# Two plain chunks instead of three in the FFN behind attention, and its root mean square taken two tiles earlier

## The reference, cut to what matters

```python
def rms_norm_2(x, g):
    y = x * lax.rsqrt(jnp.mean(x * x, axis=-1, keepdims=True) + 1e-6)
    return y * g

def swiglu(x, w_gate, w_up, w_down):
    return (jax.nn.silu(x @ w_gate) * (x @ w_up)) @ w_down

for l in range(2):                      # x is 512 tokens x 1024
    x = x + 0.5 * swiglu(rms_norm_2(x, ffn1_norm[l]), ...)      # FFN 1, hidden width 2816
    ...                                 # projections, forgetting attention, recurrence
    x = x + merged @ w_out[l]
    x = x + 0.5 * swiglu(rms_norm_2(x, ffn2_norm[l]), ffn2_w_gate[l], ffn2_w_up[l], ffn2_w_down[l])
```

## Time and profile before

| | |
|---|---|
| median of 3 runs | 3305.78 us (3305.65 to 3306.15) |
| profiled execution | 3305.81 us, of which the trace spans 3304.1 us |
| PE busy | 3288.7 us |
| DVE / ACT / POOL busy | 2273.0 / 1532.7 / 2197.9 us |
| FFN 2 of layer 0, its plain part | from 1763.79 us to the first fast matmul at 1851.32 us |
| one plain chunk of it | 1807.80 to 1840.44 us |
| one fast chunk of it | 1882.67 to 1913.28 us |

### The profile page before, as it was taken

The page is one execution under the profiler, slowest core; times in us unless marked ns, Lnnn a source line. Parts: engine busy times, 40 slices in busy tenths (PEclk is TensorE's granted clock), DMA queues, the critical chain, the costliest instruction groups (busy, mean ns, idle before and its releaser), DMA issues.

```text
span 3304.1 us, 54409 instructions
## 1 busy us (share of the span) xinstructions
PE 3288.7 (100%) x18310; PEld 2811.7 (85%) x18310; DVE 2273.0 (69%) x3503; ACT 1532.7 (46%) x2141; POOL 2197.9 (67%) x2139
## 2 busy tenths in 40 slices
PE   9999999999999999999999999999999999999999
PEld 5888778899889997788888899889987888888998
DVE  8887685988877878714435888778878334247887
ACT  4365664443443336735544333533347445534333
POOL 6443445877769886553356888689875544468896
PEclk9999999999999999999999999999999999999999
DMA  6221453322232223332223322233223222223232
GB/s 225 89 71 65 166 179 115 119 97 99 89 115 96 102 89 102 102 122 65 75 89 108 115 101 103 77 115 114 93 86 115 90 102 71 83 95 109 102 109 101
DMA packets 94488, 343.40 MB, mean 104 GB/s; under 512 B 10609, under 2 KB 11249, under 8 KB 93954
## 3 DMA queue, kind: packets, MB, share of 16 engines
q1 hardware_dynamic: 86978, 312.11, 27.5%
q10 hardware_dynamic: 7360, 29.29, 2.8%
HBM read 335.03 MB, written 2.13 MB: 102 GB/s over the span
## 4 chain that ended last, share of the span: by engine, by line
PE 85%; DVE 5%; POOL 4%; DVEq 2%; issue 2%; ACT 1%; DMA 0%; ACTq 0%; SPq 0%; POOLq 0%
PE ps L689 25%; PE ps L691 25%; PE ps L690 25%; POOL w_lo L635 3%; POOL t_lo L635 1%; PE ps L856 1%; PE ps L857 1%; PE ps L858 1%; PE ps L1391 1%; PE ps L1373 1%; PE ps L938 1%; PE ps L884 1%; DVE arena L2765 1%; PE ps L1382 1%; DVEq L2787 0%
## 5 line engine op out<-in xcount | busy, mean ns | idle before, releaser
L635 POOL TENSOR_TENSOR w_lo<-raw,w_hi 128x256 fp32r<-128x256 f32 (+1 forms) x1468 | 1306.3, 920 | 906.8 <-ACT w_hi L1479 905.1
L689 PE MATMUL ps<-a_hi,w_lo 128*128 128x512 f32 (+1 forms) x2728 | 1020.6, 374 | 1.1 <-POOL w_lo L635 0.7
L691 PE MATMUL ps<-a_hi,w_hi 128*128 128x512 f32 (+1 forms) x2728 | 1006.1, 369 | 0.0
L690 PE MATMUL ps<-a_lo,w_hi 128*128 128x512 f32 (+1 forms) x2728 | 1005.4, 369 | 0.0
L635 POOL TENSOR_TENSOR w_lo<-arena,w_hi 128x512 fp32r<-128x512 f32 x514 | 780.4, 1544 | 170.9 <-ACT w_hi L2078 114.6
L689 PEld LDWEIGHTS ps<-a_hi,w_lo 128*128 128x128 f32 x2728 | 513.4, 188 | 100.4 <-issue 18.0
L691 PEld LDWEIGHTS ps<-a_hi,w_hi 128*128 128x128 f32 x2728 | 512.4, 188 | 87.8
L690 PEld LDWEIGHTS ps<-a_lo,w_hi 128*128 128x128 f32 x2728 | 512.8, 188 | 80.8 <-issue 0.5
L1479 ACT ACTIVATE w_hi<-raw 128x1024 fp32r<-128x1024 f32 x321 | 336.6, 1053 | 324.5 <-PE ps L691 305.2
L689 PE MATMUL ps<-b_hi,w_lo 128*128 128x512 f32 (+1 forms) x1052 | 390.1, 371 | 0.6 <-POOL w_lo L635 0.2
L2078 ACT ACTIVATE w_hi<-arena 128x1024 fp32r<-128x1024 f32 x192 | 203.7, 1061 | 398.0 <-PE ps L691 398.0
(11 more groups left out here) (365 smaller groups left out, 4982.1 us busy)
## 6 DMA issues: line engine op xcount, KB each, us to landing
raw<-in_stream SPq DMA_DIRECT2D x419, 512.0 KB, 3.3
arena<-in_stream SPq DMA_DIRECT2D x148, 512.0 KB, 3.3
arena<-in_mod_w ACTq DMA_DIRECT2D x32, 512.0 KB, 4.2
arena<-in_mod_w SPq DMA_DIRECT2D x16, 512.0 KB, 11.6
arena<-arena ACTq DMA_DIRECT2D x16, 256.0 KB, 3.7
arena<-cum_rows ACTq DMA_DIRECT2D x2, 2048.0 KB, 9.6
xres<-in_x_t SPq DMA_DIRECT2D x4, 512.0 KB, 5.3
arena<-in_first SPq DMA_DIRECT2D x8, 256.0 KB, 11.8
```

The costliest lines, as they stand in the source:

```text
L635: last = pool.tensor_tensor(to[:, at], of[:, at], hi[:, at].bitcast(F32), ALU.subtract)
L689: pe.matmul(out, lo, x_hi, start=start, stop=False)
L690: pe.matmul(out, hi, x_lo, start=False, stop=False)
L691: return pe.matmul(out, hi, x_hi, start=False, stop=stop)
```

## The change

For the FFN behind attention (parts 2 and 4) the number of plain chunks falls from three to two, and the number of fast chunks rises from eight to nine. FFN 1 keeps three and eight.

- PE: `split_stats` moves from the middle of u2 to a place inside `project_fresh`, after six of its eight steps (36 of 48 matmuls). One `up` and one `down` go; one more turn of the loop of fast chunks comes.
- ACT: `inverse_rms` moves ahead of the two `tick`s in `raw_rms`. The four `round_xn` come at once after the first two silus; the four `round_turns` and the units follow in a new order (`ffn_two`).
- DVE: `ffn_two` puts the four `normalise_x` between the first scalings, `make_turns(0)` into the first up pair and `make_turns(1)`, `(2)`, `(3)` into the second, and the first weight sums into the adding of the one down product that is left.
- POOL: turn 0 stands ahead of the third unit from the end (it was the fifth), turn 1 ahead of the second, turn 2 ahead of the last.
- The PSUM banks in which the fast chunks start change with the count of tiles. No byte of the weights and no other stage changes.

```diff
-PLAIN = 3
-FAST = FFN_CHUNKS - PLAIN
+PLAIN = (None, 3, 2, 3, 2)
+FAST = [FFN_CHUNKS - n if n else None for n in PLAIN]
...
-        FAST_BANK = (None, 0, 0, 2, 0)
+        FAST_BANK = (None, 0, 2, 0, 2)
...  # POOL
-                for stop, k in zip((end - 5, end - 2, end - 1, end) if part else (end - 5, end - 4, end - 1, end), range(4)):
-                    low_run(n, stop)
+                ahead = (5, 4, 1, 0) if part == 0 else (5, 2, 1, 0) if PLAIN[part] == 3 else (3, 2, 1, 0)
+                for k, units in enumerate(ahead):
+                    low_run(n, end - units)
                     low_turns(part, k)
...  # PE
-            def project_fresh(*banks, of=OF_A):
+            def project_fresh(*banks, of=OF_A, between=None):
                 slots = [unit() for _ in banks]
                 x_hi, x_lo = of
                 for k in range(KT):
+                    if between and k == 6:
+                        between()
...
-                project_fresh(bank_a(), bank_a(), of=OF_B)
-                project(bank_v(), split_stats, OF_B)
+                project_fresh(bank_a(), bank_a(), of=OF_B, between=split_stats if second else None)
+                project(bank_v(), None if second else split_stats, OF_B)
                 project(bank_v(), of=OF_B)
-                for chunk in range(1, PLAIN):
+                for chunk in range(1, plain):
                     up()
-                    down((chunk - 1) % 2)
+                    down((plain - chunk) % 2)
...  # ACT
-            def raw_rms():
+            def raw_rms(early=False):
                 c.split.n += 1
                 c.sq.n += 1
+                if early:
+                    inverse_rms(D, sign=-1.0)
                 tick(ahead=1)
                 tick(ahead=2)
-                inverse_rms(D, sign=-1.0)
+                if not early:
+                    inverse_rms(D, sign=-1.0)
...
+            def ffn_two(next_layer):
+                gate_tiles(False)
+                for k in range(4):
+                    round_xn(k)
+                pass_v()
+                second_up(1)
+                def turned(m):
+                    if m == 0:
+                        round_turns(0)
+                        hidden_hi(1, 1)
+                    else:
+                        round_turns(1)
+                gate_tiles(True, turned)
+                if next_layer < LAYERS:
+                    load_layer(next_layer)
+                tick()
+                round_turns(2)
+                pass_v()
+                tick()
+                hidden_hi(0, 0)
+                round_turns(3)
+                pass_v()
+                first_rounds()
+                fast_chunks()
...  # DVE
+            def ffn_two(g):
+                def beside_first(n):
+                    if n == 0:
+                        normalise_x(g, 0)
+                    if n == 1:
+                        for k in range(1, 4):
+                            normalise_x(g, k)
+                    if n == 2:
+                        make_turns(0)
+                def beside_second(n):
+                    if n == 0:
+                        make_turns(1)
+                    if n == 1:
+                        make_turns(2)
+                    if n == 2:
+                        make_turns(3)
+                def beside_down(n):
+                    if n == 1:
+                        dve.wait_ge(turns_ready, 4 * c.part.n + 1)
+                        sums("gate", 0, 2, 0)
+                    if n == 4:
+                        sums("gate", 2, 3, 0)
+                    if n == 5:
+                        dve.wait_ge(turns_ready, 4 * c.part.n + 3)
+                        sums("gate", 3, 4, 0)
+                    if n == 7:
+                        sums("up", 0, 1, 0)
+                ffn_up(1, beside_first)
+                ffn_up(0, beside_second)
+                dve.drain()
+                add_tiles(ffn_out, beside=beside_down)
+                dve.memset(cols[:, 126:127], 0.0).then_inc(normalised, 1)
+                sums("up", 1, 4, 0)
+                fast_chunks()
```

More of the change, by code:

```diff
@@ L62 @@
 PARTS = 1 + 2 * 2
-TRIPS = [MLP_FAST] + [FAST] * 4
+TRIPS = [MLP_FAST] + FAST[1:]
 GROUP = [4] + [6] * 4
@@ L74 @@
 STEPS = 8 + 3
-V_TILES = (4 + 4 * 2 * 3 + 8 + 8 * MLP_CHUNKS) + LAYERS * (2 * 10 * PLAIN + 5 + 8 + 8 + 8 + 8)
+V_TILES = (4 + 4 * 2 * 3 + 8 + 8 * MLP_CHUNKS) + 10 * sum(PLAIN[1:]) + LAYERS * (5 + 8 + 8 + 8 + 8)
 FIRST = 4
@@ L80 @@
 MIXER = 16 + 24 + 16 + 16 + 8
-SEGMENTS = [(60 - FIRST + 12 + 8) + 4 * MLP_PLAIN - 2] + [2 + 6 * PLAIN - 2, 2 + MIXER + 6 * PLAIN - 2] * LAYERS + [2]
+SEGMENTS = [(60 - FIRST + 12 + 8) + 4 * MLP_PLAIN - 2] + [2 + (MIXER if part % 2 == 0 else 0) + 6 * PLAIN[part] - 2 for part in range(1, PARTS)] + [2]
 UNITS = sum(SEGMENTS)
@@ L668, in _ @@
                 end = ENDS[part]
-                for stop, k in zip((end - 5, end - 2, end - 1, end) if part else (end - 5, end - 4, end - 1, end), range(4)):
-                    low_run(n, stop)
+                ahead = (5, 4, 1, 0) if part == 0 else (5, 2, 1, 0) if PLAIN[part] == 3 else (3, 2, 1, 0)
+                for k, units in enumerate(ahead):
+                    low_run(n, end - units)
                     low_turns(part, k)
-                    n = stop
+                    n = end - units
                 with pool.Fori(0, TRIPS[part]) as i:
@@ L1232, in ffn @@
             def ffn():
+                plain = PLAIN[c.part.n]
+                second = plain == 2
                 def up():
@@ L1246, in ffn @@
                 fast_chunk(True)
-                with loop(pe, FAST - 1, c, fast_lo=LOWS[1], gate_silu=2, up_read=2, down_read=8, hid=2):
+                with loop(pe, FAST[c.part.n - 1] - 1, c, fast_lo=LOWS[1], gate_silu=2, up_read=2, down_read=8, hid=2):
                     fast_chunk(False)
@@ L1917, in raw_after_project @@
                 x_square(KT - 1)
-                raw_rms()
+                raw_rms(PLAIN[c.part.n] == 2)
             def raw_after_down(g):
@@ L2124, in second_up, with ffn_chunks @@
                 pass_v()
-            def ffn_chunks(next_layer=LAYERS):
+            def ffn_chunks():
                 def first_chunk(m):
@@ L2150, in ffn_chunks, with first_rounds @@
                 second_up(0)
+                first_rounds()
[22 more added lines that the diff above has]
+                pass_v()
+                first_rounds()
+                fast_chunks()
+            def first_rounds():
                 for u in range(2):
@@ L2159, in ffn_chunks, with fast_chunks @@
                 fast_round(2, 0)
-                c.hid.n += 2 * PLAIN
-                with loop(act, FAST - 1, c, fast=FAST_TILES, fast_raw=16, gate_sums=4, up_sums=4, gate_ready=2, hid=2):
+            def fast_chunks():
+                c.hid.n += 2 * PLAIN[c.part.n]
+                with loop(act, FAST[c.part.n] - 1, c, fast=FAST_TILES, fast_raw=16, gate_sums=4, up_sums=4, gate_ready=2, hid=2):
                     fast_chunk(False)
@@ L2397, in _ @@
                 raw_after_project("ffn2_g")
[L2398 to L2401, removed]
+                ffn_two(layer + 1)
                 if layer + 1 < LAYERS:
@@ L3214, in ffn_chunks, with fast_chunks @@
                 sums("up", 1, 4, 0)
-                dve.drain()
-                with loop(dve, FAST - 1, c, fast=FAST_TILES, fast_raw=16, fast_lo=LOWS[1], gate_silu=2):
+                fast_chunks()
+            def ffn_two(g):
[27 more added lines that the diff above has]
+                ffn_up(0, beside_second)
+                dve.drain()
+                add_tiles(ffn_out, beside=beside_down)
+                dve.memset(cols[:, 126:127], 0.0).then_inc(normalised, 1)
+                sums("up", 1, 4, 0)
+                fast_chunks()
+            def fast_chunks():
+                dve.drain()
+                with loop(dve, FAST[c.part.n] - 1, c, fast=FAST_TILES, fast_raw=16, fast_lo=LOWS[1], gate_silu=2):
                     fast_chunk(False)
@@ L3454, in _ @@
                 take_rt()
-                ffn_up(0)
-                ffn_chunks("ffn2_g")
+                ffn_two("ffn2_g")
                 if layer + 1 < LAYERS:
```

2 lines of the change are left out of this document (removed).

## The result

| | before | after |
|---|---|---|
| median | 3305.72 us (3305.46 to 3306.31, 8 runs) | 3315.58 us (3315.31 to 3316.06, 8 runs) |
| profiled execution, its span | 3305.81, 3304.1 us | 3315.83, 3314.1 us |
| PE busy | 3288.7 us | 3289.8 us |

The ratio is 1.003, with a 95% interval of 1.0019 to 1.004: 9.9 us slower, where 3315.1 was forecast.

A forecast was written before the change was run, and what follows sets the result against it. PE bounds the kernel, busy for 3288.7 of 3304.1 us. New waits of 3.5 + 1.1 + 1.4 + 0.7 = 6.7 us per FFN, less 2.03 gained, give +4.67, +9.3 for both: 3315.1 us, 8-in-10 range 3306 to 3320.

The forecast's parts named there:

- eight normalising operations: DVE's chain before the down tiles: 0.68 us each alone, 1.15 beside POOL, most slow; 7.9 us (5.4 to 9.2).
- four turns: DVE's chain before the down tiles: 5.0 us each with POOL hardly ever idle, 20.0 us (12.1 to 21.6).
- the rest of DVE's chain: Before the down tiles: four scalings 2.8 us, up tiles 6.0, three low parts of hidden tiles 3.9.
- PE's wait up to the fourth down tile: PE would start it at 48.1, but DVE frees its bank at 51.6: 3.5 us, partly showing one tile row earlier.
- first fast chunk, above 31.35: Late third weight sum makes PE wait four times for POOL's units: 1.4 us, 0.7 more than the 0.74 before.
- its own sign: Wrong if PE's idle time in each FFN is below 5 us, or turns take less than 4.5 us each.
- The cover holds: Rival: DVE's chain ends by 48.1; 3301.7 us if all is hidden, 3303 to 3306 if POOL's queue waits; chance 0.09.
- Half of it: Rival: weaker contention, DVE's chain 1.5 us shorter, sums 1.05 each, 5 us of waits; 3311 to 3312.4 us; chance 0.16.
- everything beside POOL: Rival: all DVE two-input operations run beside POOL, chain 2.9 us longer, sums 0.6; 3322.1 us; chance 0.05.
- Whole pieces: Rival: each DVE two-input operation waits for a whole POOL piece, turns near 8 us, chain 12 longer; 3339 us; chance 0.01.
- The clock falls: Rival: PE granted 1.2 instead of 2.4 GHz for the remaining down tiles, 6.8 us more per FFN; 3329 us; chance 0.03.
- The step that failed: In the clock rival: the granted clock stayed at its upper level through PE's 2.5 us wait for the first load.

The follow-up runs named there:

- the kernel that drops from both: Kernel after, in both FFNs behind attention POOL fills the turns' low parts with zeros and DVE omits the fourth turn's four sums: 3302.35 us, ratio 0.9989.
- late root mean square: Kernel after, with the sum of squares and `inverse_rms` back in their old places: 3319.01 us, ratio 1.004.
- weight sums two later: Kernel after, with DVE's first two weight sums behind the fourth adding instead of the second: 3315.17 us, ratio 1.0028.
- the last up tile ahead of the turn: Kernel after, DVE's work reordered: last up tile before the fourth turn, addings between its sums, last two low parts behind third and fourth adding: 3315.45 us, ratio 1.0028.

## Why the prediction was right

The time, the place and the mechanism came as forecast, with one exception in layer 0, told below. By its steps, from the FFN's first matmul, in layer 1, whose clock was whole (DVE's times in layer 0):

| step | forecast | measured |
|---|---|---|
| first scaling | 11.0 | 10.96 |
| eight normalising operations | 7.9 | 8.94 |
| four turns | 20.0 | 19.6 |
| the rest of DVE's chain | 12.7 | 12.2 |
| bank of the last up tile free | 51.6 | 51.7 |
| PE's wait up to the fourth down tile | 3.5 | 3.7 (1.02 of it ahead of the first) |
| ahead of the fifth | 1.1 | 1.2 |
| ahead of the seventh | 1.4 | 1.1 |
| fast chunks start | 60.9 | 61.1 |
| first fast chunk, above 31.35 | 0.7 | 0.85 |
| all waits | 6.7 | 7.0 |

The chain's length was right by two errors that cancel: normalising was 1.0 too short, the turns and the rest 0.9 too long. For the normalising the prediction took most, not all, of the operations beside POOL; seven or all eight were: the last six took 1.18 each, and POOL began 0.46 us into the first. The waits of the table add up to 6.9; the remaining 0.2 are tiles that take a little over 1.36 us behind a wait. That DVE and POOL slow each other was an inference from the earlier trace rows; that it decides here is shown now: DVE's chain is 2.8 us shorter where POOL has less to do, with DVE's work unchanged.

By its own sign the prediction was right in one FFN only. It called itself wrong if PE's idle time fell below 5 us. By the windows of the second FFN PE is idle for 5.9 us in layer 1 and for 3.9 in layer 0, which lost as much time (7.2 us against 7.0): there the clock fell, and PE was slow where it would have been idle. The prediction had no such path; that its sum held in layer 0 too is luck as far as it goes, and what the windows show of it stands below, with the clock. The small waits in the first fast chunk came at the fourth and seventh unit (0.42 and 0.40 us), forecast at the third to sixth.

The rivals. *The cover holds* fell: neither the turns on DVE nor those on POOL had room, and only the kernel that drops from both gets to 3302.35. *Half of it* and *everything beside POOL* are off by 3 us and more. *Whole pieces* fell with the steps of the turns, 0.80 to 0.81. The Trainium skill (SBUF — State Buffer, section SBUF: two separate sides) has the lock held for the full instruction; the trace of after disagrees as that of before did: a step takes 0.80 us, not the over 1.1 that the prediction worked out from that rule.

*The clock falls* was given 0.03, and there the prediction was right about the time and wrong about the chip. The granted clock did fall, in one of the two FFNs. Windows of PE in layer 0: the third tile's end and the wait, the fourth tile, the fifth, the sixth and seventh, up to the fast chunks.

```profile
1811.72:1815.64 3.92, 1.56 (x7) 0.94 (x6) 3.54 (x5) 2.02 (x3) 3.92 (x6) 1.00 0.00 0
1815.64:1818.17 2.53, 1.98 (x6) 1.08 (x7) 1.78 (x3) 0.62 (x1) 2.53 (x4) 0.74 0.44 105
1818.17:1820.86 2.69, 2.69 (x6) 2.14 (x7) 2.44 (x3) 0.00 (x0) 2.69 (x4) 0.50 0.24 96
1820.86:1823.42 2.56, 2.56 (x7) 2.01 (x6) 2.36 (x4) 1.06 (x1) 2.45 (x3) 0.50 0.00 0
1823.42:1826.31 2.89, 2.89 (x13) 2.38 (x12) 2.56 (x4) 0.00 (x0) 2.25 (x2) 0.96 0.01 6
```

PE had been busy for 1.56 of the 3.92 us before it resumed at 1815.64; during the fourth tile the clock went to 0.50, the lower of the two levels, 1.2 GHz. The fifth tile took 2.69 us where it took 1.45 in layer 1. The fast chunks started 1.37 us later than in layer 1. But the priced 6.8 us did not come: the first fast chunk was then 1.19 us shorter (31.01 against 32.20), since in layer 1 PE waits in it for POOL, and the whole stretch differs by 0.18. So it is in the other kernels with two plain chunks, where the fall came in one FFN and not the other:

| first matmul to end of first fast chunk | with a fall | without |
|---|---|---|
| after | 93.44 (layer 0) | 93.26 (layer 1) |
| late root mean square | 94.99 (layer 0) | 95.20 (layer 1) |
| weight sums two later | 92.28 (layer 1) | 92.63 (layer 0) |

The pairs differ by 0.4 us at most, and the stretch with a fall is the shorter one in two of three: its end is set by DVE's and POOL's supply, and a slower PE spends time that it would have waited. What a fall costs where nothing else holds PE up, no run here shows.

The step that failed is the reason for the 0.03: that the clock had stayed at its upper level through the wait of 2.5 us at the kernel's start. The slices of 83 us can't show it. Short windows say 1.00 there too (9.73 to 10.58, for one), but the matmuls behind that wait don't agree with them: of one line and shape, they start 0.85 us apart up to 10.58 and 0.43 apart from 11.22 on. In the FFN a clock of 0.50 had the same effect, 0.43 us from one matmul to the next for 0.23. From the timeline of PE in the kernel before, instruction by instruction:

```profile
9.73 1.06 PE L872 MATMUL ps<-arena,ones 128*128 128x512 f32 x1
10.58 0.80 PE L872 MATMUL ps<-arena,ones 128*128 128x512 f32 x1
11.22 0.59 PE L872 MATMUL ps<-arena,ones 128*128 128x512 f32 x1
11.65 0.61 PE L872 MATMUL ps<-arena,ones 128*128 128x512 f32 x1
```

So that place was no evidence for a whole clock. Whether it really was at its lower level there, without the row saying so, stays open.

The expectation for the late root mean square (2 to 4.7 us for each FFN, likeliest 3321) missed at 1.7 us, for the reason shown there.

## What to carry to other kernels

Before giving an engine's slack away, add up its neighbour's too: where two engines slow each other, as DVE and POOL do here, idle time of the one keeps the other fast, and a chain moved earlier may move into the other's work. A wait that two queues share (here turns owed by DVE and POOL) was not removed by reordering one of them; take work from both, or find the small waits that a better order of the existing slack can pay. Look at the clock in windows of a few microseconds around each new wait, and ask whether PE or its supply ends the stretch before pricing a fall. Check the granted clock against the time from one matmul to the next of the same shape.

## What the runs showed of the hardware that was not expected

- The granted clock fell to its lower level behind single waits of about 2.4 us (2.36 in layer 0) and, with the last up tile ahead of the turn, behind 3.63 and 2.78 us (0.58 and 0.59 over the 4.00 us that follow). In the windows above it is back after some 7 us, with the weight sums two later after less than 5. It is not a fixed answer to the wait: in layer 1 of the kernel after, PE waits 2.39 us at the same place and the clock stays 1.00; with the weight sums two later it is the other way round, a fall in layer 1 behind 2.37 us and none in layer 0 behind 2.36. Where no wait in the FFN was over 1.5 us, none fell. What tells the two cases apart stays open.
- DVE's two-input operations with one operand in PSUM aren't slowed beside POOL: in the chain above L3119 and L3123 take 0.70 and 0.69 while POOL works, and L3129, which has both in SBUF, takes 1.05 right before them; where POOL is idle, in the kernel without the turns' low parts, the same takes 0.69.
- The loss is on both sides: DVE's six normalising operations and POOL's eight pieces take 4.05 and 6.10 us when the six come behind the eight, 7.05 and 8.45 when nearly all of the six stand beside POOL's.
